# The order of a recurrence unit written anew in a one-core encoder layer: transposes, key preparation and scores placed elsewhere

## The reference, cut to what matters

```python
def step(state, inp):
    r_t, w_t, k_t, v_t, kk_t, a_t = inp
    sa = jnp.einsum('bhvk,bhk->bhv', state, kk_t)
    state = (state * w_t[:, :, None, :]
             - sa[..., None] * (kk_t * a_t)[:, :, None, :]
             + v_t[..., None] * k_t[:, :, None, :])
    return state, jnp.einsum('bhvk,bhk->bhv', state, r_t)
...
y = (rwkv7_scan(r_h, decay_h[0], k_dir[0], v_h, kk, a_h[0], reverse=False)
     + rwkv7_scan(r_h, decay_h[1], k_dir[1], v_h, kk, a_h[1], reverse=True))
```

## Time and profile before

| | |
|---|---|
| median of three runs | 1598.67 us (1598.45 to 1601.05) |
| profiled execution | 1600.05 us, its span 1598.3 us |
| mean granted TensorE clock | 0.983 |
| busy | PE 1455.2 us (91%), PEld 729.4 (46%), DVE 510.2 (32%), ACT 240.0 (15%), POOL 177.5 (11%) |
| the recurrence's units | from 269.5 to 540 us of the span |

### The profile page before, as it was taken

One profiled execution on the slowest core, in us unless ns is written; L12 is line 12 of the kernel. 1 busy time (PEld: TensorE's weight loads), 2 busy tenths in 40 slices (PEclk: granted clock), 3 DMA queues, 4 the chain that ended last, 5 costly groups with the idle time before them and its releaser, 6 DMA issues.

```text
span 1598.3 us, 26196 instructions
## 1 busy us (share of the span) xinstructions
PE 1455.2 (91%) x11376; PEld 729.4 (46%) x11376; DVE 510.2 (32%) x712; ACT 240.0 (15%) x478; POOL 177.5 (11%) x349
## 2 busy tenths in 40 slices
PE   8999999888897995899989989989989989989977
PEld 6344455878886653434324324324324324324322
DVE  6666534666674564001101101101101101101103
ACT  3333321112212121100000000000000000000002
POOL 1323504433333110000000000000000000000000
PEclk9999999999999997899999999999999999999999
DMA  9245577766766635499999999999999999999994
GB/s 302 66 159 187 187 257 168 174 132 133 143 113 136 262 166 210 192 428 423 422 427 425 424 426 426 423 427 426 425 425 427 424 425 427 425 425 427 423 424 184
DMA packets 186070, 500.47 MB, mean 313 GB/s; under 512 B 125904, under 2 KB 135248, under 8 KB 153216
## 3 DMA queue, kind: packets, MB, share of 16 engines
q1 hardware_dynamic: 180192, 479.31, 78.4%
q0 software_dynamic: 5792, 19.88, 3.6%
HBM read 470.83 MB, written 28.33 MB: 312 GB/s over the span
## 4 chain that ended last, share of the span: by engine, by line
PE 32%; DMA 24%; DVE 2%; issue 1%; ACT 1%; DVEq 0%; SPq 0%
DMA ring<-in_exp_w_up 24%; PE pD L1557 14%; PE pG L1518 6%; PE pU L1538 6%; PE pX L1506 4%; PE pG L1538 3%; DVE res L1666 1%; DVE hid L1684 1%; PE pX L1545 1%; ACT hidT L1627 0%; DVE res L1702 0%; ACT xin L1610 0%; PE pX L1574 0%; ACT xin L1642 0%; ACT L1645 0%
## 5 line engine op out<-in xcount | busy, mean ns | idle before, releaser
L1684 DVE TENSOR_TENSOR hid<-silu,pU 128x512 f32<-128x512 f32 x32 | 20.6, 684 | 774.9 <-PE pU L1538 774.9
L1538 PE MATMUL pU<-ring,xin 128*64 128x512 f32 x768 | 173.8, 597 | 37.5 <-DMA ring<-in_exp_w_up 37.5
L1538 PE MATMUL pG<-ring,xin 128*64 128x512 f32 x768 | 171.3, 595 | 11.5 <-DMA ring<-in_exp_w_gate 10.8
L1557 PE MATMUL pD<-ring,hidT 128*64 128x512 f32 x768 | 167.9, 593 | 2.1 <-ACT hidT L1627 2.1
L1518 PE MATMUL pG<-yexp,scatter 128*128 128x512 f32 x256 | 124.4, 618 | 3.5 <-DVE res L1666 1.9
L1538 PEld LDWEIGHTS pU<-ring,xin 128*64 128x64 f32 x768 | 52.3, 137 | 157.5 <-issue 92.3
L1538 PEld LDWEIGHTS pG<-ring,xin 128*64 128x64 f32 x768 | 53.0, 137 | 116.8 <-issue 97.6
L1557 PEld LDWEIGHTS pD<-ring,hidT 128*64 128x64 f32 x768 | 55.4, 137 | 107.7 <-issue 107.0
L1666 DVE TENSOR_TENSOR res<-res,pG 128x512 f32<-128x512 f32 x128 | 86.9, 686 | 45.9 <-PE pG L1518 45.9
L1518 PEld LDWEIGHTS pG<-yexp,scatter 128*128 128x128 f32 x256 | 40.6, 188 | 87.1 <-DVE res L1666 62.9
L1506 PEld LDWEIGHTS pX<-pick,y 128*128 128x128 f32 x512 | 60.2, 197 | 5.4 <-issue 3.3
(11 more groups left out here) (238 smaller groups left out, 1731.1 us busy)
## 6 DMA issues: line engine op xcount, KB each, us to landing
ring<-in_exp_w_gate SPq DMA_DIRECT2D x48, 2048.0 KB, 34.6
ring<-in_exp_w_up SPq DMA_DIRECT2D x48, 2048.0 KB, 27.8
ring<-in_exp_w_down SPq DMA_DIRECT2D x48, 2048.0 KB, 28.8
lent_slot<-in_exp_w_up SPq DMA_DIRECT2D x16, 2048.0 KB, 20.5
lent_slot<-in_exp_w_gate SPq DMA_DIRECT2D x16, 2048.0 KB, 31.8
lent_slot<-in_exp_w_down SPq DMA_DIRECT2D x16, 2048.0 KB, 33.8
lent_slot<-in_rw_w_in SPq DMA_DIRECT2D x8, 1024.0 KB, 12.8
scratch_sw<-tok POOLq DMA_DIRECT2D x8, 512.0 KB, 3.9
```

Source lines behind the costliest of these rows:

```text
L1538: mm = pe.matmul(psum[f // 2][HEAD * s:HEAD * s + HEAD, :], xin[:, k, e, :], w[:, FF * r + HALF * f:FF * r + HALF * f + HALF], start=k == ...
L1557: mm = pe.matmul(pD[h][HEAD * s:HEAD * s + HEAD, :], hidT[:, j, c, HEAD * s:HEAD * s + HEAD], w[:, 4 * half + 2 * s + c % 2, HALF * h:HALF ...
L1684: dve.tensor_tensor(hid[:, j, :], silu[:, j, :], pU[j][:, :], ALU.mult).then_inc(hid_done, 1)
```

## The change

No operation is added or taken away; the order on PE and on DVE is another one. On PE all four `turn_keys` parts move ahead of the level 0 fills: two between the halves of N X, two behind them. Each group of scores moves up: group 0 stands before `sum_state(n, 0)` instead of behind `sum_r_state(n, 1)`, the other three follow two, two and one blocks later, and the last comes before `sum_state(n, 1)`. `cumulate` now comes before each `sum_y`, so that `sum_y(n, 1)` is the last block of a unit. On DVE the `queries` of unit n + 3 stand at the end of unit n (those of unit 2 before the loop); before, those of unit n + 2 stood behind `cross` at the start of unit n. `removed_keys` comes behind each pair of level 0 additions, `added_keys` around the level 1 `cross`, and the masks start right behind `removed(n, 0)`. The orders of ACT, SP and POOL are not touched.

```diff
--- before.py
+++ after.py
@@ -974,18 +974,19 @@
                     pe.wait_ge(inv_ev, FILLS * n)
                     pe.wait_ge(r_ev, 2 * n)
                 fill(n, 0, 0, scored(n), of(X))
+                turn_keys(n, (0, 1))
                 pe.wait_ge(v_in[n % 2], V_SUM * (n // 2 + 1))
                 if n:
                     for e in range(2):
                         pe.wait_ge(u_ev[e], 2 * n)
                 fill_with_values(n)
+                turn_keys(n, (2, 3))
                 for g in range(2):
                     pe.wait_ge(inv_ev, FILLS * n + 1 + g)
                     if n:
                         pe.wait_ge(y_ev, 2 * n - 1 + g)
                     fill(n, 2 + g, g, of(XT[n % 2]), of(W))
                     fill(n, g, g, of(W), of(XT[n % 2]))
-                    turn_keys(n, (2 * g, 2 * g + 1))
                 sum_r_state(n, 0)
                 for g in range(2):
                     pe.wait_ge(inv_ev, FILLS * n + 3 + 2 * g)
@@ -997,32 +998,33 @@
                     pe.wait_ge(s_ev, steps_summed(n - 1))
                 solve_u(n, 0)
                 sum_r(n, 1)
+                if ahead:
+                    scores(n + 2, 0)
                 for e in range(2):
                     pe.wait_ge(u_ev[e], 2 * n + 1)
                 pe.wait_ge(tk_ev, 4 * (n + 1))
                 sum_state(n, 0)
                 sum_y_state(n, 0)
+                if ahead:
+                    scores(n + 2, 1)
                 pe.wait_ge(s_ev, steps_summed(n - 1) + 1 if n else 1)
                 sum_r_state(n, 1)
-                if ahead:
-                    scores(n + 2, 0)
                 sum_y_state(n, 1)
                 if ahead:
-                    scores(n + 2, 1)
+                    scores(n + 2, 2)
                 solve_u(n, 1)
                 if ahead:
-                    scores(n + 2, 2)
+                    scores(n + 2, 3)
                 for e in range(2):
                     pe.wait_ge(u_ev[e], 2 * n + 2)
                 if ahead:
                     sum_state(n, 1)
-                    scores(n + 2, 3)
+                if n + 3 < UNITS:
+                    cumulate(n + 3, (0, 1))
                 sum_y(n, 0)
                 if n + 3 < UNITS:
-                    cumulate(n + 3, (0, 1))
+                    cumulate(n + 3, (2, 3))
                 sum_y(n, 1)
-                if n + 3 < UNITS:
-                    cumulate(n + 3, (2, 3))
 
         @block.vector
         def _(dve):
@@ -1116,6 +1118,8 @@
                     masked(n, g)
             dve.wait_ge(cleared, 2)
             dve.wait_ge(v_out[2], 16)
+            for k in range(2):
+                queries(2, k)
             for n in range(UNITS):
                 ahead = n + 2 < UNITS
                 if n == LAST:
@@ -1123,35 +1127,32 @@
                     head_norm(dve, keep, 0)
                 for g in range(2):
                     cross(n, 0, g, g, 1 + g)
-                if ahead:
-                    for k in range(2):
-                        queries(n + 2, k)
                 for g in range(2):
                     add_to(n, X, g, 2 + g, 3 + 2 * g)
                     add_to(n, XT[n % 2], g, g, 4 + 2 * g)
+                    if ahead:
+                        removed_keys(n + 2, g)
                 if ahead:
-                    removed_keys(n + 2, 0)
+                    added_keys(n + 2, 0)
                 for g in range(2):
                     cross(n, 1, g, 2 + g, 7 + g)
+                if ahead:
+                    added_keys(n + 2, 1)
                 for g in range(2):
                     add_to(n, XT[n % 2], g, g, 9 + g)
-                if ahead:
-                    removed_keys(n + 2, 1)
                 removed(n, 0)
                 if ahead:
-                    added_keys(n + 2, 0)
+                    masked(n + 2, 0)
                 add_state(n, 0)
                 if n == LAST:
                     scale_and_add(dve, keep, 0, v_last)
                 if ahead:
-                    added_keys(n + 2, 1)
-                    masked(n + 2, 0)
                     masked(n + 2, 1)
+                    masked(n + 2, 2)
                 removed(n, 1)
                 if ahead:
-                    masked(n + 2, 2)
+                    masked(n + 2, 3)
                     add_state(n, 1)
-                    masked(n + 2, 3)
                 add_y(n, 0)
                 add_y(n, 1)
                 if ahead:
@@ -1160,6 +1161,9 @@
                     dve.wait_ge(s_ev, 2 * n + 2)
                     dve.tensor_tensor(S[b][0][:, :, :], carry[b][:, :, :], step_on[:, :].unsqueeze(2).to_broadcast([P, DC, HEAD]),
                                       ALU.mult).then_inc(state_ready, 1)
+                if n + 3 < UNITS:
+                    for k in range(2):
+                        queries(n + 3, k)
 
 
 WEIGHT_BLOCKS = 6
```

## The result

The changed kernel takes 1606.24 us in the median (1605.74 to 1609.07, five runs) against 1598.67; the ratio is 1.0048, 95% interval 1.0033 to 1.0063. It is 7.6 us slower, where 1599.0 was forecast, and lies outside the range. The profiled execution took 1605.81 us, its span is 1604.0 us (5.7 more), the mean granted clock 0.980 (0.983 before).

What follows compares the result with a forecast made beforehand. PE was taken to bound the recurrence, expert-weight DMA the rest from 540 us. First part +8.5, keys +2.8, second part -4.4, unit 5 -0.9, cover of other gaps 5.7: +0.3 us, put on the median as 1599.0; range 1594 to 1605.

Steps and rivals of the forecast that it cites:

- First part of a unit: Unit start to `solve_u`: DVE's added work delays it by 1.8 us in units 1 to 4, 1.3 in unit 0.
- U+4.2: U is a unit's start; 4.2 us later PE was to be ready for the level 0 fills, then wait 0.35.
- cover: PE's issue gaps hidden by new waits for DVE in or just before them: 6.3 us taken, bounds 0 and 9.4.
- The rival named for a slower result: At the first level 1 fill, DVE's waits and the gaps both stay: 1602.5 to 1608 us, named 1604; chance 0.23.
- the gaps: PE pauses put down to "issue", differing by unit, up to 2.19 us; guessed to be instruction fetching in blocks of 256.
- Its second half, the clock: PE's new waits could bring stretches at 0.50 of the clock, about 1.6 us each, 0 to +3; within the 0.23.
- keys: At `removed_keys`, the keys' DMA lands near U+8.0, 0.7 us after DVE wants them: 2.8 us in units 1 to 4.
- second part: From `solve_u(n, 0)` on: 0.66 us gained in units 0, 1 and 4, 1.23 in 2 and 3; 4.4 in all.
- The U wait: PE's 0.57 us before `sum_state(n, 0)` for DVE's copy of U; to go, gaining only in units 2, 3 and 5.
- those of score groups 1 and 2: PE's waits for masks before these groups, 0.37 and 0.29 us a unit; to go, with two blocks ahead of them.
- From unit 5 to unit 7: End of the recurrence: unit 7's first fill moves with the last mask of unit 5, by -0.9 us.
- the rival: POOL pays: `base` growing over 3.4 us a unit makes PE wait at every start, +1 to +5 us; chance 0.03.

Runs made afterwards that it cites:

- run 6: Changed kernel with transposes, `cumulate` and `queries` put back and DVE's key operations re-placed, early scores and masks kept: 0.9955 to the kernel before, 1594.87 us.
- run 7: Kernel before with only DVE's four key operations moved, both `removed_keys` behind all level 0 additions, `added_keys` around the last additions: 1.0000 to the kernel before.
- run 2: Kernel before with only the key transposes moved, in all units: 1.0053 to the kernel before.
- run 4: Changed kernel with SP storing the last tile of value rows before it waits for the blocks: 1.0013 to the kernel before.
- run 8: Changed kernel with the early store of value rows and both `removed_keys` behind the level 0 additions, `added_keys` around the last additions: 0.9992 to the kernel before.
- run 1: Changed kernel with the key transposes back behind the level 0 fills in unit 0 alone: 1.0038 to the kernel before.
- run 3: Kernel before with only the key transposes moved, in all units but unit 0: 1.0017 to the kernel before.
- run 9: Changed kernel with the early store of value rows, and SP loading the keys of unit n + 3 ahead of the blocks: 1.0066 to the kernel before.
- run 10: The kernel of run 6 with SP loading the keys of unit n + 3 ahead of the blocks: 1.0042 to the kernel before.

## Why the prediction was wrong

**The step that failed** is in "First part of a unit": "In unit 0 the queries lie ahead of the loop and no `add_y` precedes them, so `cross` comes 0.5 earlier: 1.3." The moved transposes entered it only as PE work ("PE, with the four transposes moved ahead, is ready at 4.2"); PE's wait for ACT, which reads them, stood in the sum at nothing. In unit 0 PE came to the level 0 fills at U+10.1, not at U+4.2, because ACT may not write TK before the store of the value rows has landed. The row of before was there to be read: 5.75 us of ACT's wait for that store. For unit 0 the sum had about -0.2 us (1.3, less 0.66 and 0.85 of cover). Measured +6.9: this wait took 4.7 more than before, and the clock behind it 2.4. In the profiled executions the forecast was +0.3 and the spans say +5.7. Unit 0 is 7.1 over, units 1 to 4 are 1.2 under, the end 0.4 under. The medians lie another 1.8 us further apart than the profiled executions, which is within the scatter of single executions (1597.7 to 1601.2 us for the kernel before). What a moved block costs is known only when each engine that reads it has been asked what it waits for at the new time; I asked that only of DVE.

**The rival named for a slower result has the size, not the cause.** It was to be slower because the gaps stay beside DVE's waits, from a cover under 3.4 us on. In units 2 and 4 they did stay (3.5 and 1.9 us before, 3.3 and 1.8 after), in 1 and 3 they went (3.4 to 1.8, 1.3 to 0): 3.1 us of cover where 4.9 were forecast. Even so units 1 to 4 lost nothing in sum. Its second half, the clock, did occur, in unit 0 behind a pause of PE for another reason.

**Units 1 to 4: right in sum, by misses that cancel.** Forecast: first part 4 x 1.8 and keys 4 x 0.7, together +10.0; second part -3.8, cover -4.9; so +1.3. Measured +0.1. Up to `solve_u(n, 0)`, where PE's work is the same, the four units took 59.3 us before and 70.2 after, +10.9. Of that 6.9 are waits for DVE, 1.2 more gaps in this part and 2.8 the rest, in which most of the new half-clock stretches lie (10.2 us of them in these units against 3.4). Behind it they took 83.8 and 73.0, -10.8. The waits for masks fell by 2.6 and those for U by 1.1, together 3.7 as forecast; the gaps there, 4.3 us, all went; the half-clock stretch of unit 1 went too; one to two us aren't placed. The keys were mis-sized: DVE waited 0.75, 0.90, 2.53 and 1.60 us for them, 5.8 instead of 2.8, because they landed at U+8.1, 8.2, 9.9 and 8.9 instead of 8.0.

**What the profile was to show**, one by one. The U wait and those of score groups 1 and 2 are gone, group 3 waits 0.30 and `cumulate` 0.38 in unit 4 (forecast 0.3 and 0.4). At the first level 0 fill PE waits 0.25 in each unit (0.35). At the first level 1 fill that waits for `cross` it is 0.30, 0.51, 2.55 and 1.21 in units 1 to 4 (1.3 to 2.0); where a gap stood just ahead of it, the wait was the shorter, and unit 3, without a gap, has 2.55 and another 1.44 for X. At `solve_u` 0.58 and 0.31 in units 1 and 2, none in 3 and 4 (0.4). `removed_keys` waits for the DMA in all four, as forecast. There are eight issue gaps in the recurrence instead of twelve. The first fill of unit 7 waits 6.31 (7 or more). From unit 5 to unit 7 it is -0.9, to the tenth, and that is luck: the last mask came 2.1 us earlier in the unit instead of 0.9, and the chain from there to the first fill took 33.2 us instead of 32.1. POOL's 32 steps are busy 51.9 us in units 1 to 4 instead of 46.7, 1.3 more a unit, where the rival needed more than 3.4; that POOL would get something back when the queries leave did not show.

**The gain of the early scores has the forecast size**: 4.4 us for units 0 to 4, and in unit 5 the waits (0.57 + 0.37 + 0.29) and one block (1.1), together 6.7 us. Runs 6 and 7 differ by them alone, and by 0.45%, 7.2 us. Part of the match is luck, since by the account of run 7 it is made up of other terms too. **The loss sits in parts priced at nothing or too low**: moving the transposes costs 0.53% alone (run 2, priced at 0), the early scores give back some of it, and key operations between the additions may cost again, some 3 us by runs 4 and 8, whose intervals overlap. The new places of `queries` and `cumulate` had no run of their own; run 1 shows that the queries ahead of `cross` can hold PE for 2.10 us.

**What the issue gaps go with.** The traces keep the packets of the queue that loads instructions (`q8 instruction`, 16 KB each, one every 3 to 8 us in units 1 to 4). All 12 gaps of 0.45 us or more in the kernel before, and all 8 in the changed one, end 1.2 to 1.8 us after such a packet has landed; in the 14 traces together it is 115 gaps and 1.0 to 2.0 us. For the gap of 1.93 us that ends at 428.51 the packet starts at 426.14 and lands at 427.21. Of the three pauses of 0.57 before `sum_state` only one does so (0.34, 0.81 and 1.41 us after a landing), which agrees with their being waits for U. Most packets have no gap behind them (in units 1 to 4 of the kernel before 25 packets and 8 gaps). So the gaps go with the loading of instructions, as the prediction had guessed from their spacing; no run has tested that they are caused by it.

What stays open: why only some packets have a gap behind them, and whether gaps shrink because PE waits nearby (a fetcher that runs on is argued, not shown); where the 0.17% of run 3 lies; what `queries` and `cumulate` cost in their new places; and how much of the 3.1 us of gaps would have gone anyway.

## What to carry to other kernels

Before a block is moved ahead in an order, ask of every engine that reads its output what that engine waits for at the new time, and do it for the first pass through the loop by itself, where buffers are still lent to the stage before. A long wait on an engine off the path that costs its neighbours 0.2 us is a warning, not a comfort: note what covers it, since the next edit may take the cover away. When two edits are bundled (here early scores, which gain 7 us, and early transposes, which lose 8), take the profile apart by unit before judging either. And when one of them is undone, look at the waits again: others of the new order can step into its place, as in run 1.

## What the runs showed of the hardware

- A pause of PE of 4.94 us was followed by 6.8 us at 0.50 of the clock, which cost 2.4 us more; with the pause at 0.76 us the clock stayed at 1.00 in this unit. In unit 4 a stretch with PE busy for 1.24 of 3.40 us was followed by the same 6.8 us. The stall in unit 0 cost half its length again.
- With two transfers of the keys in front of it on SP's queue, the small strided write of the blocks took 7.4 to 8.6 us until its read-back could be issued, instead of 4.8 to 6.8 (run 9 against 4); with none in front 6.2 and 6.3.
- Every gap of at least 0.45 us that is put down to "issue" in the small-matmul stage, but for the pauses of 0.5 to 0.6 before `sum_state`, ended 1.0 to 2.0 us after a 16 KB packet of the instruction queue had landed (115 gaps, 14 traces).
- All waits put down to "issue" in the recurrence added up to 4.0 and 5.1 us in the two runs whose first fills wait 20.9 and 30.0 us for XT (runs 9 and 10), and 8.7 or more in all others. Over units 1 to 4 the gaps fell from 10.1 to 7.0 us in the changed kernel. That waiting makes them shrink is a reading of these figures, not a tested one.
